# Transformer step in fp32: the weight sums of the gate/up products by accumulating DMAs in place of GpSimd

## What is computed

```python
def rms_norm(x, g):
    y = xf * lax.rsqrt(jnp.mean(xf * xf, axis=-1, keepdims=True) + EPS)
    return (y * g.astype(jnp.float32)).astype(x.dtype)

def swiglu(h, w_gate_up, w_down):
    gu = h @ w_gate_up
    g, u = gu[..., :D_FF], gu[..., D_FF:]
    return (jax.nn.silu(g) * u) @ w_down

# in trunk, for each of the two layers
        x = x + mix
        x = x + swiglu(rms_norm(x, norm_ffn_g[i]), w_gate_up[i], w_down[i])
```

## Time and profile before

| | us |
|---|---|
| median of 3 runs | 1784.37 |
| the runs | 1782.86 to 1786.16 |
| the profiled execution, its own time | 1783.48 |
| span in its trace, first to last instruction | 1781.7 |
| TensorE busy | 1681.9 |
| VectorE busy | 1163.0 |
| ScalarE busy | 749.7 |
| GpSimd busy | 510.0 |

### The profile page before, as it was taken

The page is one execution under the profiler, slowest core; times in us unless marked ns, Lnnn a source line. Parts: engine busy times, 40 slices in busy tenths (PEclk is TensorE's granted clock), DMA queues, the critical chain, the costliest instruction groups (busy, mean ns, idle before and its releaser), DMA issues.

```text
span 1781.7 us, 33276 instructions
## 1 busy us (share of the span) xinstructions
PE 1681.9 (94%) x14036; PEld 1549.3 (87%) x14036; DVE 1163.0 (65%) x1409; ACT 749.7 (42%) x1271; POOL 510.0 (29%) x325
## 2 busy tenths in 40 slices
PE   7999899999889999999999998999899999999998
PEld 7999666689889999999999995666899999999998
DVE  6663366667994598378632327777689946983883
ACT  5443355565442244134342206666455423441431
POOL 0000100004772386056000000000057714850660
PEclk9999999999999999999999999999999999999999
DMA  5125799921222122212223339998112221222222
GB/s 187 69 98 214 285 382 380 379 107 48 93 74 95 48 95 72 95 49 94 95 95 130 130 120 369 377 369 341 63 56 72 87 101 50 72 96 71 71 96 83
DMA packets 38463, 258.74 MB, mean 145 GB/s; under 512 B 4528, under 2 KB 4656, under 8 KB 9264
## 3 DMA queue, kind: packets, MB, share of 16 engines
q1 hardware_dynamic: 34560, 245.15, 37.1%
q0 software_dynamic: 3760, 11.54, 1.9%
HBM read 242.51 MB, written 13.11 MB: 143 GB/s over the span
## 4 chain that ended last, share of the span: by engine, by line
PE 61%; DVE 14%; POOL 11%; issue 9%; ACT 4%; DMA 0%; ACTq 0%; SPq 0%; DVEq 0%
PE ps L545 28%; PE ps L730 6%; POOL t L842 5%; DVE s_lo L700 4%; PE ps L257 4%; PE ps L258 4%; PE ps L259 4%; POOL t L844 3%; PE ps L1219 3%; POOL sg L858 2%; PE ps L1170 2%; PE ps L1123 2%; PE ps L581 2%; DVE up L944 2%; PE ps L1139 1%
## 5 line engine op out<-in xcount | busy, mean ns | idle before, releaser
L700 DVE TENSOR_TENSOR s_lo<-t,s_hi 128x512 fp32r<-128x512 f32 x176 | 207.2, 1188 | 16.8 <-ACT s_hi L696 16.5
L257 PE MATMUL ps<-w_hi,h_hi 128*128 128x256 f32 x640 | 183.1, 286 | 11.5 <-DVE h_lo L289 10.4
L235 DVE TENSOR_TENSOR w_lo<-w_raw,w_hi 128x2048 fp32r<-128x2048 f32 x55 | 126.0, 2291 | 98.9 <-ACT w_hi L227 89.1
L700 DVE TENSOR_TENSOR s_lo<-w_raw,s_hi 128x512 fp32r<-128x512 f32 x132 | 183.7, 1392 | 1.1 <-ACT s_hi L696 1.1
L258 PE MATMUL ps<-w_lo,h_hi 128*128 128x256 f32 x640 | 182.0, 284 | 0.0
L259 PE MATMUL ps<-w_hi,h_lo 128*128 128x256 f32 x640 | 182.0, 284 | 0.0
L227 ACT ACTIVATE w_hi<-w_raw 128x2048 fp32r<-128x2048 f32 x55 | 105.0, 1909 | 162.9 <-PE ps L545 154.5
L611 DVE TENSOR_TENSOR xT<-ps,xT 128x640 f32<-128x640 f32 x64 | 52.7, 823 | 180.4 <-PE ps L545 169.7
L696 ACT ACTIVATE s_hi<-t 128x512 fp32r<-128x512 f32 x176 | 108.6, 621 | 139.2 <-PE ps L730 68.1
L545 PE MATMUL ps<-gu_hi,w_hi 128*128 128x320 f32 x704 | 161.0, 310 | 6.2 <-issue 4.4
L730 PE MATMUL ps<-hs_hi,s_hi 128*128 128x320 f32 x528 | 163.6, 310 | 0.0
(11 more groups left out here) (244 smaller groups left out, 4303.2 us busy)
## 6 DMA issues: line engine op xcount, KB each, us to landing
w_raw<-in_w SPq DMA_DIRECT2D x99, 1024.0 KB, 4.8
kv<-in_k_s SPq DMA_DIRECT2D x30, 1024.0 KB, 7.9
kv<-in_v_a SPq DMA_DIRECT2D x18, 1024.0 KB, 8.0
work<-in_v_s SPq DMA_DIRECT2D x16, 1024.0 KB, 8.2
kv<-in_k_a SPq DMA_DIRECT2D x14, 1024.0 KB, 8.3
work<-in_v_a SPq DMA_DIRECT2D x14, 1024.0 KB, 8.6
extra<-in_k_a SPq DMA_DIRECT2D x8, 1024.0 KB, 7.2
w_raw<-in_k_a SPq DMA_DIRECT2D x8, 1024.0 KB, 8.7
```

The source lines that it names most:

```text
L235: nc.vector.tensor_tensor(w_lo[s][:, :, :], w_raw[:, s, :, :], w_hi[s][:, :, :].bitcast(F32), ALU.subtract).then_inc(lo_done, 1)
L257: nc.tensor.matmul(out, s_hi, m_hi, start=first, stop=False, skip_group_check=True)
L700: nc.vector.tensor_tensor(s_lo[i][:, :, :], factor(j % 2, i), s_hi[i][:, :, :].bitcast(F32), ALU.subtract)\
```

## The change

It does three things, all in the feed-forward.

1. The four weight sums of a gate/up unit are no longer made by GpSimd instructions but by DMAs that add their source to what stands in the destination (`accum_op=ALU.add`), issued from GpSimd's queue: `sum1` adds block 0 onto block 1 in `w_raw` itself, `sum2` adds that onto `t2` (which SyncE has loaded with a copy of block 2), `sum3` adds block 2 onto `t3` (loaded with block 1), `sum4` adds `t2` onto `t4` (loaded with block 3). SyncE therefore has three more loads of 256 KB for each unit (`load_next`), and frees `w_raw` after block 5 instead of 6.
2. A DMA only adds here, so all differences became sums; the signs are moved into the activations (`neg_gains`, `odd_dve`), and the up block comes out negated.
3. The second factor 1/rms is gone from `scale`; `product` now waits for SiLU itself, and the residual after each down unit is two VectorE instructions: PSUM times `rstd_row` into `sg`, then `xT` minus that. The orders of `ffn_act`, `ffn_pool` and `ffn_dve` are rewritten: `product` and `split_gu` now stand earlier in VectorE's order.

```diff
         def factor(s, i):
-            return (raw_block(s, 0), t2[:, :, :], t13[:, 0], raw_block(s, 3), t13[:, 1], raw_block(s, 2), t4[:, :, :])[i]
+            return (raw_block(s, 0), t2[s][:, :, :], raw_block(s, 1), raw_block(s, 3), t3[:, :, :], raw_block(s, 2),
+                    t4[:, :, :])[i]
...
             if i in (0, 3, 5):
                 raw_ready(act, g, j, j % 2)
             else:
-                act.wait_ge(ff["t"], 3 * v + {2: 1, 4: 1, 1: 2, 6: 3}[i])
+                act.wait_ge(sums[{2: "w1", 1: "w2", 4: "w3", 6: "w4"}[i]], 16 * (v + 1))
...
-            def factor13(g, j, v):
+            def sum1(g, j, v):
                 raw_ready(pool, g, j, j % 2)
...
-                nc.gpsimd.tensor_tensor(out, b0[:, 512:1536], b0[:, 0:1024], ALU.subtract).then_inc(ff["t"], 1)
-                pool.wait_ge(ff["t"], 3 * v + 1)
-                nc.gpsimd.tensor_tensor(t2[:, :, :], raw_block(j % 2, 2), t13[:, 0], ALU.subtract)\
-                    .then_inc(ff["t"], 1)
...
-                nc.gpsimd.tensor_tensor(t4[:, :, :], raw_block(j % 2, 3), t2[:, :, :], ALU.subtract)\
-                    .then_inc(ff["t"], 1)
+                settle(pool)
+                nc.gpsimd.dma_start(raw_block(j % 2, 1), raw_block(j % 2, 0), accum_op=ALU.add)\
+                    .then_inc(sums["w1"], 16)
+
+            def sum2(g, j, v):
+                pool.wait_ge(sums[f"t2{'ab'[j % 2]}"], 16 * (v // 2 + 1))
+                pool.wait_ge(sums["w1"], 16 * (v + 1))
+                settle(pool)
+                nc.gpsimd.dma_start(t2[j % 2][:, :, :], raw_block(j % 2, 1), accum_op=ALU.add).then_inc(sums["w2"], 16)
+
+            def sum3(g, j, v):
+                raw_ready(pool, g, j, j % 2)
+                pool.wait_ge(sums["t3"], 16 * (v + 1))
+                settle(pool)
+                nc.gpsimd.dma_start(t3[:, :, :], raw_block(j % 2, 2), accum_op=ALU.add).then_inc(sums["w3"], 16)
+
+            def sum4(g, j, v):
+                pool.wait_ge(sums["t4"], 16 * (v + 1))
+                pool.wait_ge(sums["w2"], 16 * (v + 1))
+                settle(pool)
+                nc.gpsimd.dma_start(t4[:, :, :], t2[j % 2][:, :, :], accum_op=ALU.add).then_inc(sums["w4"], 16)
...
-            def scale(v, s):
-                pool.wait_ge(ff["silu"], v + 1)
-                nc.gpsimd.tensor_tensor(sg[:, s, :], sg[:, s, :], rstd_row, ALU.mult).then_inc(ff["sr"], 1)
...
             def product(v, s):
-                dve.wait_ge(ff["sr"], v + 1)
+                dve.wait_ge(ff["silu"], v + 1)
...
-                    nc.vector.tensor_tensor(x, banks(OUT[n]), x, ALU.add).then_inc(x_done, 1)
+                    x, y = halves(xT[:, 2 * j + n, :]), banks(OUT[n])
+                    if ch is not None:
+                        ch.link(nc.vector.tensor_tensor(halves(sg[:, n, :]), y, halves(rstd_row), ALU.mult))
+                        nc.vector.tensor_tensor(x, x, halves(sg[:, n, :]), ALU.subtract).then_inc(x_done, 1)
+                    else:
+                        nc.vector.tensor_tensor(x, y, x, ALU.add).then_inc(x_done, 1)
...
+                elif u - 2 in gu_units:
+                    sp_.wait_ge(lo_done, splits[u - 2] - 1)
                 elif u > 1:
                     sp_.wait_ge(lo_done, splits[u - 2])
...
+            def load_next(u):
+                if u - 1 in gu_units:
+                    v, j, g = gu_units[u - 1]
+                    if v % N_F != 0:
+                        sp_.wait_ge(lo_done, gu_split(v - 1, 4))
+                    sp_.dma_start(t3[:, :, :], block(u - 1, 1)).then_inc(sums["t3"], 16)
+                load(u, u % 2)
+                if u - 1 in gu_units:
+                    if v % N_F != 0:
+                        sp_.wait_ge(lo_done, gu_split(v - 1, 6))
+                    sp_.dma_start(t4[:, :, :], block(u - 1, 3)).then_inc(sums["t4"], 16)
+                if u in gu_units:
+                    v, j, g = gu_units[u]
+                    if v % N_F == 0:
+                        sp_.wait_ge(mm, tiles_before(unit_before(g), 1))
+                    elif v > 1:
+                        sp_.wait_ge(sums["w4"], 16 * (v - 1))
+                    sp_.dma_start(t2[j % 2][:, :, :], block(u, 2)).then_inc(sums[f"t2{'ab'[j % 2]}"], 16)
```

## The result

The changed kernel takes **1832.8 us** (median of 4 runs, 1830.1 to 1836.9) against 1785.3 us before: ratio 1.027, with a 95% interval of 1.024 to 1.029. The forecast was 1730, in a range of 1724 to 1785. It is slower by 48 us where a gain of 54 was forecast. The profiled run of after has a span of 1828.4 us, 46.7 more than before.

What follows compares the result with a forecast made beforehand. TensorE's gate/up waits, nearly all for u3 held up by GpSimd's sums, were taken as the bound. 53.6 won there, plus 1.7 at chunk ends, less 0.8 for the residual, gave 54.5 us off: 1730, range 1724 to 1785.

Steps and rivals of the forecast that it cites:

- What bounds the kernel, and what is to be won: Gate/up stages: TensorE waits for u3, late through GpSimd, ScalarE and VectorE; 29.7 us lost in a layer, 59.4 in all.
- The new ring through `u3`: Gate/up unit: u3 through GpSimd, ScalarE and VectorE back to u3 takes 10 us with handovers, below TensorE's 12.3.
- The start of the first chunk: First chunk: TensorE's 3.0 us wait and the clock's loss go; an estimated 1.3 us wait in unit 1 stays.
- End of a last chunk, residual: Last chunk's down unit: 1.7 us won; extra VectorE residual instruction hidden except in the kernel's last tile, 0.8 us lost.
- SyncE: "about 5.7 us into a unit ... It fits with 2 us": SyncE's loads: t4 and t2 land behind the 1 MB load, about 5.7 us into a unit; sum4's followers fit with 2.
- L = 4.2 and the 0.9 beside it: Adding DMAs on GpSimd's queue: 4.2 us from issue to landing, 0.9 us for an issue; ring of 9.3 us, hidden.
- the formula: GpSimd's queue of adding DMAs: a unit's ring is 2L + 0.9 us, L being the time from issue to landing.
- Rival A: Adding DMAs' ring too long: landings of 7.5 us make it 15.9, costing 115 us, time 1845; chance 0.18.
- Rival B: Landings of 5.7 to 6.6 us, or late sum2, hold up ScalarE before copy_p5: 0.9 us over 32 places, 1758; chance 0.14.

Runs made afterwards that it cites:

- both-orders kernel: The changed kernel with sum1 and sum2 issued earlier on GpSimd, and copy_p5 and u3 ahead of what waits for sums: 1748.1 us, ratio 0.981.

## Why the prediction was wrong, step by step

- **What bounds the kernel, and what is to be won**: right. 59.4 us of losses; with GpSimd's sums cut small, 51.9 us were won, and the stages of layer one, 100.5, 99.5 and 75.0 us, were within 1 us of the forecast's 101.5, 99 and 74.3.
- **The new ring through `u3`**: right in itself. Splits have a median of 0.69 us, as foretold, though that is no proof of the reason given, since they have 0.68 in the kernel with the new order and the sums still on GpSimd. The 13.3 us that TensorE still waits for `u3` follow a stop at product 5, since VectorE does `u3` behind the late block 1.
- **The start of the first chunk**: half right. The 3.0 us of the earlier trace rows went, and 2.2, 1.7 and 0.7 us came for `copy_p1`, `copy_p5` and `u3`. The clock didn't come back, 0.97 for 0.98.
- **End of a last chunk, residual**: right. The down unit behind it takes 49.64 us for 50.53, and 42.77 for 43.65: 1.8 us won, 1.7 forecast. The last tile has two VectorE instructions of 0.82 us in place of one.
- **SyncE: "about 5.7 us into a unit ... It fits with 2 us"**: the first step that failed. It put `t4`'s load right behind the 1 MB load. In fact it is issued 2.6 us later in the unit shown, when block 6 is split, and takes 7.8 us more until GpSimd has it: 10.4 us behind the large load, and 8.6 to 9.7 in the three units before, where the prediction had 5.7 us into the unit. The text named what stands behind `sum4`, and priced the slack with a wrong landing. With it went the next claim, that in the middle of a unit nobody else waits on SyncE: ScalarE and TensorE do, through `sum4`, `sum1` and `sum2`.
- **L = 4.2 and the 0.9 beside it**: the second. One value was taken for four sums: 3.3, 4.3, 7.1 and 7.3 us were measured. The median of `vnew`, 6.2, set aside because its stretch is busier, was nearer for the two that run beside a 1 MB load. Yet this is the smaller fault: with the medians of the two sums that stand in that ring, 4.3 and 7.1, the formula gives 12.3 us, TensorE's own time. The rest of its 14.85 us is the 2.7 us of issues and hand-overs that stood there as 0.9. What the sum needed was not the mean load of the engines but what runs at the moment of issue.
- **Rival A** had the sign and nearly the time (1845), and the time was luck. Its ring exists, but A had L = 7.5 for both landings and 0.9 for the rest, and it knew nothing of `t4`'s load, which ended 31 of the 40 waits of `sum4`. **Rival B** had the mechanism, a late `sum2` with `copy_p5` behind it on ScalarE, and priced it at 0.9 us a unit; it is 2.8 in the units shown, as the ring closes over two units. The chances of both together, 0.32, were too low, and they should have been one case: a late sum and the queue behind it lengthen each other.
- **Not priced at all**: the lower clock behind new stops. TensorE was busy for 7.9 us more in layer one with the same matmuls, PEld for 5.7.

The Trainium skill ("Collectives: The Full Stack", "The bandwidth ceiling") gave adding DMAs half the rate. The trace bears it out where the engines are shared, 7.6 against 4.1 us for `sum2`, and in the engines' time that GpSimd's queue took: 14.4 points over the kernel before with adding, 6.8 without. Where the engines are free it is less, 3.3 against 2.3 us.

What stays open: which of the two rings through `sum4` costs how much, since every run that breaks one also touches the other; and how much of the 75 us between the two ways of summing each order is worth alone in each layer. Layer two of the both-orders kernel has a stop of 4.3 us for `copy_p1` in its first chunk which layer one hasn't, and I have no run for that.

## What to carry to other kernels

When work moves from an engine to DMAs, draw the ring through every in-order queue that it passes: who waits to issue, what is ahead of it, what stands behind the waiter; then place what doesn't depend on the transfer ahead of it. Price a transfer by what runs beside it when it is issued, one price for each, and not by the mean share of the DMA engines. And leave room in the price of a stop of TensorE for slower matmuls behind it.

## What I had not expected of the hardware

- A 256 KB sum within SBUF takes 3.3 us (`sum4`), and 6.7 to 7.6 us at the median where it is issued just behind a 1 MB load (`sum2`, 0.2 to 1.3 us behind it in the units looked at).
- A 256 KB load lands in 3.5 us at the median ahead of the 1 MB load in SyncE's queue (`t3`), and in 6.4 us behind it (`t4`). With 8 KB in place of 256 in all but the first units it is 2.2 and 5.3 us: the place costs some 3 us, the size about 1.
- GpSimd's issue of a sum is an instruction of 0.86 to 0.88 us at the median, 1.2 for `sum1`, four times a unit, and at 17% busy GpSimd still held the kernel, by waiting.
